# Feed-forward input products: seven block products instead of eight, on one Trainium2 core

## The chip, the cores and the metric

The kernel is one launch on one core of a Trainium2 chip. The metric is the device time of the launch in microseconds, the median of several runs. TensorE (PE) multiplies, VectorE (DVE), ScalarE (ACT) and GpSimd (POOL) work element by element, SyncE (SP) issues the weight transfers.

## What is computed

A two-layer encoder for 512 prompt frames and 64 sample frames, 576 columns in all, of width 1024. Each layer has two feed-forward blocks around a mixer (retention in the first layer, forgetting attention in the second). Only the feed-forward block matters here:

```python
gate, up = jnp.split(rmsnorm(h, g) @ w_in, 2, axis=-1)   # w_in: 1024 x 5632
h = h + 0.5 * (silu(gate) * up) @ w_out                  # w_out: 2816 x 1024
```

There are four such blocks, called ffn1_0, ffn2_0, ffn1_1 and ffn2_1. Before ffn2_0 runs the output product of retention, before ffn1_1 the key and value products (sections k and v), before ffn2_1 the output product of attention (fox_out).

## The kernel before

Activations lie transposed: 128 features on the partitions, the 576 columns (T) along the free axis, eight such tiles for h (KD = 8). A unit is one output tile of 128 features: `unit` (L1543) runs over its kt blocks of 128 inputs, and `product` (L1532) makes three matmuls of 288 columns for each block and column half: low weight by high input, high by low, high by high, because each fp32 value is split into two fp32r parts. A unit of eight blocks is 48 matmuls. A feed-forward block has 44 input units, a gate and an up unit for each of the 22 hidden tiles, and its output units run in two parts (FF_PARTS: 10 and 12 hidden tiles), after the input units of the part.

Per unit SP loads the fp32 tile into `raw` (L459), ACT casts it to `wh` (`split_hi`, L597) when the unit two earlier has left PE, DVE subtracts to get `wl` (`split_lo`, L602), and PE waits for that. `section` (L605) puts these splits two units ahead of each unit's eviction. The evictions of a pair: DVE multiplies the gate by the normaliser `rstd` (L989), ACT applies silu (L650), POOL multiplies by `rstd` (L1437), DVE multiplies with the up unit in PSUM (L993), ACT casts (L652) and DVE subtracts (L996), which gives `acth` and `actl` for the output units. Output units are added into h by `take_h` (L962); in the last part ACT scales h by the next gain (`x_tile`, L639), DVE makes its low part (L917), and POOL sums squares (`sum_squares`, L1411, L1418). PE adds the partitions (L1573), DVE takes the root by Newton steps (`token_rstd`, L920) and PE spreads it (L1582), from within the first units of the next section. Everything is ordered by program order on each engine and by semaphores.

## Time and profile before

| | |
|---|---|
| median of 3 runs | 2560.07 us |
| runs | 2559.99 to 2560.84 us |
| the profiled execution | 2560.84 us, its span 2560.8 us |
| PE busy | 2529.7 us |
| DVE, ACT, POOL busy | 1054.5, 697.4, 338.6 us |

The page gives busy time for each engine and a picture of the span in 40 slices. The durations of single instructions come from the trace; those of matmuls overlap one another, so their cost is read from start to start. Duration and start-to-start differ on DVE and ACT too: an instruction whose waits are met starts before the previous one has ended.

### The profile page before, as it was taken

The numbers are of one execution on the slowest core, as the hardware profiler recorded it, in microseconds if no ns is written. First come the engines' busy times: TensorE is split into PE (matmuls) and PEld (weight loads), VectorE is DVE, ScalarE is ACT, GpSimd is POOL, SyncE is SP. The second block draws the span as 40 slices with busy tenths as digits, with TensorE's granted clock in tenths as the row PEclk, the third lists the DMA queues.
The fourth block names the chain that finished last, engine by engine and source line by source line (L and its number), as shares of the span: only waits on it lengthen the run. The fifth ranks groups of instructions, "written<-read, shape, count | busy, mean of one in ns | idle before, by whom it ended". The sixth has DMA issues, their size and how long they took to land.

```text
span 2560.8 us, 44069 instructions
## 1 busy us (share of the span) xinstructions
PE 2529.7 (99%) x18791; PEld 2459.6 (96%) x18791; DVE 1054.5 (41%) x1556; ACT 697.4 (27%) x994; POOL 338.6 (13%) x266
## 2 busy tenths in 40 slices
PE   8999999999999999999999999999999999999998
PEld 8999999989898989999999999999998789999998
DVE  4333334554545555333333343323335754333332
ACT  4222222121313233222222232212223542212221
POOL 0100113210101103100113211001121021100112
PEclk9999999999999999999999999999999999999998
DMA  5222232222223122322232442322324322322231
GB/s 151 85 81 82 82 103 77 81 79 67 88 66 95 57 69 83 92 80 83 82 103 64 138 115 83 89 77 82 99 78 113 114 76 79 88 78 81 85 104 38
DMA packets 394198, 221.71 MB, mean 87 GB/s; under 512 B 8593, under 2 KB 386545, under 8 KB 394065
## 3 DMA queue, kind: packets, MB, share of 16 engines
q1 hardware_dynamic: 389328, 205.22, 27.8%
q0 software_dynamic: 4544, 14.50, 1.7%
q8 instruction: 106, 1.74, 0.3%
q14 instruction: 28, 0.22, 0.0%
q10 hardware_dynamic: 192, 0.04, 0.0%
HBM read 206.01 MB, written 13.71 MB: 86 GB/s over the span
## 4 chain that ended last, share of the span: by engine, by line
PE 96%; DVE 2%; ACT 1%; DMA 0%; issue 0%; SPq 0%; POOL 0%; ACTq 0%; DVEq 0%; POOLq 0%
PE ps L1536 88%; PE ps L1914 1%; PE ps L1719 1%; PE ps L1705 1%; PE ps L1707 1%; PE ps L1706 1%; PE ps L1942 1%; PE ps L1966 1%; DVE wl L602 0%; PE ps L1819 0%; PE ps L1698 0%; PE ps L1739 0%; DVE xl L917 0%; ACT wh L597 0%; DMA xtok<-in_x_sample 0%; PE ps L1778 0%
## 5 line engine op out<-in xcount | busy, mean ns | idle before, releaser
L602 DVE TENSOR_TENSOR wl<-raw,wh 128x1024 fp32r<-128x1024 f32 (+3 forms) x352 | 446.6, 1269 | 1266.5 <-ACT wh L597 1266.1
L1536 PE MATMUL ps<-xh,wl 128*128 128x288 f32 x4000 | 859.9, 297 | 5.9 <-DVE xl L917 4.1
L1536 PE MATMUL ps<-xh,wh 128*128 128x288 f32 x4000 | 852.1, 294 | 0.0
L1536 PE MATMUL ps<-xl,wh 128*128 128x288 f32 x4000 | 851.9, 294 | 0.0
L597 ACT CAST wh<-raw 128x1024 fp32r<-128x1024 f32 (+3 forms) x352 | 375.8, 1068 | 1146.6 <-PE ps L1536 1145.5
L1536 PEld LDWEIGHTS ps<-xh,wl 128*128 128x128 f32 x4000 | 641.2, 188 | 11.9 <-DVE xl L917 4.8
L1536 PEld LDWEIGHTS ps<-xh,wh 128*128 128x128 f32 x4000 | 642.1, 188 | 0.0
L1536 PEld LDWEIGHTS ps<-xl,wh 128*128 128x128 f32 x4000 | 641.9, 188 | 0.0
L1536 PE MATMUL ps<-actl,wh 128*128 128x288 f32 x1408 | 300.9, 294 | 0.0
L1536 PE MATMUL ps<-acth,wl 128*128 128x288 f32 x1408 | 300.4, 295 | 0.0
L1536 PE MATMUL ps<-acth,wh 128*128 128x288 f32 x1408 | 298.7, 293 | 0.0
L1437 POOL TENSOR_TENSOR rsilu<-silu,rstd 128x576 f32<-128x576 f32 x88 | 125.7, 1429 | 1244.7 <-ACT silu L650 1244.7
L1536 PEld LDWEIGHTS ps<-acth,wh 128*128 128x128 f32 x1408 | 225.2, 188 | 0.0
L1536 PEld LDWEIGHTS ps<-actl,wh 128*128 128x128 f32 x1408 | 224.6, 188 | 0.0
L1536 PEld LDWEIGHTS ps<-acth,wl 128*128 128x128 f32 x1408 | 224.2, 187 | 0.0
L650 ACT ACTIVATE silu<-gate 128x576 f32<-128x576 f32 x88 | 60.4, 686 | 186.3 <-DVE gate L989 186.2
L652 ACT CAST acth<-prod 128x576 f32 (+1 forms) x88 | 59.3, 674 | 183.9 <-DVE prod L993 183.9
L996 DVE TENSOR_TENSOR actl<-prod,acth 128x576 f32 (+1 forms) x88 | 66.7, 758 | 78.2 <-ACT acth L652 78.2
L962 DVE SCALAR_TENSOR_TENSOR h<-ps,h 128x576 f32<-128x576 f32 x104 | 78.0, 750 | 14.3 <-PE ps L1536 14.3
L917 DVE SCALAR_TENSOR_TENSOR xl<-h,gains,xh 128x576 fp32r<-128x576 f32 x56 | 56.5, 1020 | 44.3 <-ACT xh L639 33.0
L1411 POOL TENSOR_TENSOR sq<-h 128x576 f32<-128x576 f32 x37 | 45.4, 1226 | 201.4 <-DVE h L962 201.2
L993 DVE TENSOR_TENSOR prod<-ps,rsilu 128x576 f32<-128x576 f32 x88 | 66.0, 750 | 4.7 <-POOL rsilu L1437 4.7
(247 smaller groups left out, 1667.4 us busy)
## 6 DMA issues: line engine op xcount, KB each, us to landing
raw<-in_ffn_w_in SPq DMA_DIRECT2D x176, 512.0 KB, 3.8
raw<-in_ffn_w_out SPq DMA_DIRECT2D x32, 768.0 KB, 4.8
raw<-in_ret_w_in SPq DMA_DIRECT2D x48, 512.0 KB, 3.9
raw<-in_ffn_w_out SPq DMA_DIRECT2D x32, 640.0 KB, 4.4
raw<-in_ret_w_out SPq DMA_DIRECT2D x32, 256.0 KB, 2.7
raw<-in_fox_w_kvf SPq DMA_DIRECT2D x16, 512.0 KB, 4.0
raw<-in_fox_w_q SPq DMA_DIRECT2D x8, 512.0 KB, 5.4
bias<-cum_scratch SPq DMA_DIRECT2D x16, 256.0 KB, 3.4
```

The source lines that it names most:

```text
L597: nc.scalar.copy(wh[:, s % SPLIT, 0:kt, :], raw[:, s, 0:kt, :]).then_inc(hi_ready, 1)
L602: nc.vector.tensor_tensor(wl[:, s % SPLIT, 0:kt, :], raw[:, s, 0:kt, :], wh[:, s % SPLIT, 0:kt, :].bitcast(F32), ALU.subtract).then_inc(lo ...
L650: nc.scalar.activation(silu[:, s // 2, :], gate[:, s // 2, :], ACT.Silu).then_inc(silu_ready, 1)
L652: nc.scalar.copy(acth[:, 2 * i + s // 2, :], prod[:, s // 2, :]).then_inc(act_hi, 1)
L917: nc.vector.scalar_tensor_tensor(xl[:, j, :], h[:, j, :], gains[:, gain + j:gain + j + 1], xh[:, j, :].bitcast(F32), ALU.mult, ALU.subtrac ...
L962: nc.vector.scalar_tensor_tensor(h[:, j, :], unit_psum(s, ring), scale, h[:, j, :], ALU.mult, ALU.add).then_inc(taken, 1)
L993: nc.vector.tensor_tensor(prod[:, b, :], unit_psum(s, DEEP), rsilu[:, b, :], ALU.mult) \
L996: nc.vector.tensor_tensor(actl[:, 2 * i + b, :], prod[:, b, :], acth[:, 2 * i + b, :].bitcast(F32), ALU.subtract).then_inc(act_ready, 1)
L1411: nc.gpsimd.tensor_tensor(out[:, :], h[:, j, :], h[:, j, :], ALU.mult).then_inc(sq_step, 1)
L1437: nc.gpsimd.tensor_tensor(rsilu[:, b, :], silu[:, b, :], rstd[:, :], ALU.mult) \
L1536: mm = nc.tensor.matmul(out[:, a:z], w, x[:, a:z], start=start and n == 0, stop=stop and n == len(terms) - 1)
L1705: nc.tensor.matmul(out, al, bh, start=start, stop=False)
```

## The change

The gate and up tile of one hidden tile form a 2 x 2 block product: rows gate and up, inner halves the even and the odd input blocks, columns the two halves of 288. It is made by the Winograd form of Strassen's scheme with seven products of 128 x 512 by 512 x 288: 84 matmuls in place of 96, named G11, S2, S1, S3, G12, S4, U22. Four of them need sums of weight quarters (`weight_sums`, DVE), three need sums of input quarters (`x_mix`, DVE). All seven weights of a group are split (`factor_hi` on ACT, `factor_lo` on DVE) into a ring with one place per product, so the part for the next group can be made when PE has left that product of the current one. The products of a group share banks, and PE waits in the group for ACT's copy of G11 and for DVE's sums. The three parts now have 8, 8 and 6 hidden tiles. The gate is multiplied by `rstd` before silu (POOL), the up tile stays without it, and `take_scaled` multiplies by it when an output unit is evicted, in two DVE instructions. During the last four units of the section before, `lead` makes the first group's weights. In the retention section's end, fox_out and the v section the inputs are scaled (`fetch`), mixed and split pair by pair.

```diff
-TA = 288
+TA = T // 2
...
-FF_PARTS = [(0, 10), (10, 12)]
+FF_PARTS = [(0, 8), (8, 8), (16, 6)]
+LAST = len(FF_PARTS) - 1
...
+G11, S2, S1, S3, G12, S4, U22 = range(7)
+ENTRY = [4, 5, 6, 0, 1, 2, 3]
+RING = 7
+BANK = [0, 1, 2, 3, 0, 2, 3]
+SUMS = [S1, S2, S3, S4]
+FACTORS, STEPS = 7, 5
...
+            def load_pair(g, row, src):
+                s = (2 * g + row) % RAW
+                units = next((opening[a] for a in (g, g - 1) if a in opening), None)
+                if units is None:
+                    sp.wait_ge(factor_ready, FACTORS * (g - 2) + U22 + row)
+                elif units:
+                    sp.wait_ge(lo_ready, units - RAW + s + 1)
+                sp.dma_start(raw[:, s, :, :], src).then_inc(pair_in[s], 16)
...
+        def factor_hi(act, g, i):
+            units = opening.get(g)
+            if units is None:
+                act.wait_ge(made, FACTORS * (g - 1) + i + 1)
+            elif units:
+                if i < S3:
+                    act.wait_ge(made, FACTORS * g)
+                    act.wait_ge(unit_done, units - KD + 1)
+                else:
+                    act.wait_ge(unit_done, units - (1 if i < S4 else 0))
+            if i in SUMS:
+                act.wait_ge(sums_ready, 4 * g + SUMS.index(i) + 1)
+            else:
+                act.wait_ge(pair_in[(2 * g + (i == U22)) % RAW], 16 * (g // 2 + 1))
+            nc.scalar.copy(entry(wh, i), source(g, i)).then_inc(fhi_ready, 1)
+        def factor_lo(dve, g, i):
+            dve.wait_ge(fhi_ready, FACTORS * g + i + 1)
+            nc.vector.tensor_tensor(entry(wl, i), source(g, i), entry(wh, i).bitcast(F32), ALU.subtract) \
+                .then_inc(factor_ready, 1)
+        def weight_sums(dve, g, which):
+            a11, a12, a21, a22 = [quarter(g, row, col) for row in range(2) for col in range(2)]
+            s1, s2, s3, s4 = [ws[:, n, :, :] for n in range(4)]
+            for n in which:
+                if n == 0:
+                    dve.wait_ge(pair_in[(2 * g) % RAW], 16 * (g // 2 + 1))
+                    dve.wait_ge(pair_in[(2 * g + 1) % RAW], 16 * (g // 2 + 1))
+                if g:
+                    dve.wait_ge(factor_ready, FACTORS * (g - 1) + SUMS[n] + 1)
+                if n != 2:
+                    dve.wait_ge(sums_ready, 4 * g + n)
+                out, in0, in1, op = ((s1, a21, a22, ALU.add), (s2, s1, a11, ALU.subtract),
+                                     (s3, a11, a21, ALU.subtract), (s4, a12, s2, ALU.subtract))[n]
+                nc.vector.tensor_tensor(out, in0, in1, op).then_inc(sums_ready, 1)
+        def lead_lo(dve, g, which):
+            if which == 0:
+                weight_sums(dve, g, range(4))
+            for f in ((G11, S2, S1), (S3, G12), (S4, U22))[which]:
+                factor_lo(dve, g, f)
+            if which == 2:
+                weight_sums(dve, g + 1, range(4))
...
+            def fetch(n, q, ready, plain=True, rows=range(2)):
+                index = x_index[n, q, plain]
+                for r in rows:
+                    j = 2 * q + r
...
+                    gain = (G_FFN1, G_FFN2)[n % 2] + KD * (n // 2)
+                    nc.scalar.activation(xf[:, index % 2, r, :], h[:, j, :], ACT.Copy, scale=gains[:, gain + j:gain + j + 1]) \
+                        .then_inc(xf_ready, 1)
+            def x_hi(n, q, plain=True, turned=True):
+                index = x_index[n, q, plain]
+                if plain:
+                    act.wait_ge(mixed, mix_before[index] + (2 if turned else 1))
+                    nc.scalar.copy(xh[:, 2 * q:2 * q + 2, :], xf[:, index % 2, :, :]).then_inc(xfhi_ready, 1)
+                if turned:
+                    act.wait_ge(mixed, mix_before[index] + 4)
+                    nc.scalar.copy(xmh[:, q, :, :], mix[:, index % 2, :, :]).then_inc(xfhi_ready, 1)
...
+                    def activated(i):
+                        act.wait_ge(prod_ready, g0 + i + 1)
+                        nc.scalar.copy(acth[:, i, :], up[:, (g0 + i) % 2, :]).then_inc(act_hi, 1)
+                    for i in range(n):
+                        g = g0 + i
+                        more = [g + 1] if i < n - 1 else []
+                        act.wait_ge(made, FACTORS * g + G11 + 1)
+                        if g:
+                            act.wait_ge(stepped, STEPS * (g - 1) + 1)
+                        nc.scalar.copy(p1[:, :], ps[:, 4 * (g % 2) + BANK[G11], 0:TA]).then_inc(p1_ready, 1)
+                        for a in more:
+                            factor_hi(act, a, G11)
+                            factor_hi(act, a, S2)
...
+                        if i:
+                            activated(i - 1)
+                        for a in more:
+                            for f in (S1, S3):
+                                factor_hi(act, a, f)
+                        act.wait_ge(made, FACTORS * g + G12 + 1)
+                        if g >= 2:
+                            act.wait_ge(prod_ready, g - 1)
+                        nc.scalar.copy(gate[:, g % 2, 0:TA], ps[:, 4 * (g % 2) + BANK[G12], 0:TA]).then_inc(gate1_ready, 1)
+                        for a in more:
+                            for f in (G12, S4):
+                                factor_hi(act, a, f)
+                        if not more:
+                            split_hi(act, u1, u1 // 4, 0, n)
+                        act.wait_ge(gate_ready, g + 1)
+                        nc.scalar.activation(gate[:, g % 2, :], gate[:, g % 2, :], ACT.Silu).then_inc(silu_ready, 1)
+                        for a in more:
+                            factor_hi(act, a, U22)
+                    activated(n - 1)
+                    split_hi(act, u1 + 1, u1 // 4, 1, n)
...
+            def x_mix(n, q, plain=True, turned=True):
+                index = x_index[n, q, plain]
+                even, odd, m = xf[:, index % 2, 0, :], xf[:, index % 2, 1, :], mix[:, index % 2, :, :]
+                dve.wait_ge(xf_ready, 2 * index + 2)
+                if turned:
+                    nc.vector.tensor_tensor(m[:, 0, :], even[:, TA:T], even[:, 0:TA], ALU.subtract).then_inc(mixed, 1)
+                nc.vector.tensor_tensor(even[:, TA:T], odd[:, TA:T], even[:, TA:T], ALU.subtract).then_inc(mixed, 1)
+                if turned:
+                    dve.wait_ge(mixed, mix_before[index] + 2)
+                    nc.vector.tensor_tensor(m[:, 1, :], even[:, TA:T], even[:, 0:TA], ALU.add).then_inc(mixed, 1)
+                    dve.wait_ge(mixed, mix_before[index] + 3)
+                    nc.vector.tensor_tensor(m[:, 2, :], odd[:, 0:TA], m[:, 1, :], ALU.subtract).then_inc(mixed, 1)
+            def x_lo(n, q, plain=True, turned=True):
+                index = x_index[n, q, plain]
+                if plain:
+                    dve.wait_ge(xfhi_ready, plain_at[n, q])
+                    nc.vector.tensor_tensor(xl[:, 2 * q:2 * q + 2, :], xf[:, index % 2, :, :],
+                                            xh[:, 2 * q:2 * q + 2, :].bitcast(F32), ALU.subtract).then_inc(xfactor_ready, 1)
+                if turned:
+                    dve.wait_ge(xfhi_ready, mixed_at[n, q])
+                    nc.vector.tensor_tensor(xml[:, q, :, :], mix[:, index % 2, :, :], xmh[:, q, :, :].bitcast(F32),
+                                            ALU.subtract).then_inc(xfactor_ready, 1)
...
+            def take_scaled(u, s, j, gain, ring, held=up):
+                dve.wait_ge(unit_done, u + 1)
...
+                nc.vector.scalar_tensor_tensor(y, unit_psum(s, ring), 0.5, rstd[:, :], ALU.mult, ALU.mult).then_inc(scaled, 1)
+                dve.wait_ge(scaled, n_scaled[0])
+                nc.vector.tensor_tensor(h[:, j, :], h[:, j, :], y, ALU.add).then_inc(taken, 1)
+                if gain is not None:
+                    x_tile(j, gain)
...
+                    def gated(i):
+                        g, b = g0 + i, (g0 + i) % 2
+                        dve.wait_ge(silu_ready, g + 1)
+                        dve.wait_ge(stepped, STEPS * (g + 1))
+                        nc.vector.tensor_tensor(up[:, b, :], up[:, b, :], gate[:, b, :], ALU.mult).then_inc(prod_ready, 1)
+                    def activated(i):
+                        g, b = g0 + i, (g0 + i) % 2
+                        dve.wait_ge(act_hi, g + 1)
+                        nc.vector.tensor_tensor(actl[:, i, :], up[:, b, :], acth[:, i, :].bitcast(F32),
+                                                ALU.subtract).then_inc(act_ready, 1)
+                    for i in range(n):
+                        g, b = g0 + i, (g0 + i) % 2
+                        more = [g + 1] if i < n - 1 else []
+                        norm = part == 0 and i == 0
...
+                        for a in more:
+                            factor_lo(dve, a, G11)
+                        made_to(S2)
+                        dve.wait_ge(p1_ready, g + 1)
+                        if g:
+                            dve.wait_ge(stepped, STEPS * g)
+                        nc.vector.tensor_tensor(u2[:, :], bank(S2), p1[:, :], ALU.add).then_inc(stepped, 1)
+                        for a in more:
+                            factor_lo(dve, a, S2)
+                        made_to(S1)
+                        dve.wait_ge(stepped, STEPS * g + 1)
+                        nc.vector.tensor_tensor(u5[:, :], bank(S1), u2[:, :], ALU.add).then_inc(stepped, 1)
+                        if i:
+                            gated(i - 1)
+                        made_to(S3)
+                        dve.wait_ge(stepped, STEPS * g + 2)
+                        if g >= 2:
+                            dve.wait_ge(act_ready, g - 1)
+                        nc.vector.tensor_tensor(up[:, b, TA:T], bank(S3), u5[:, :], ALU.add).then_inc(stepped, 1)
+                        if norm and roots is not None:
+                            roots()
+                        for a in more:
+                            factor_lo(dve, a, S1)
+                            factor_lo(dve, a, S3)
...
+                        if i:
+                            activated(i - 1)
+                        for a in more:
+                            factor_lo(dve, a, G12)
+                        if i < n - 2:
+                            weight_sums(dve, g + 2, range(3))
+                        if not more:
+                            split_lo(dve, u1, None, 0, n)
+                        if norm and scales is not None:
+                            scales()
+                        made_to(S4)
+                        if g >= 2:
+                            dve.wait_ge(prod_ready, g - 1)
+                        nc.vector.tensor_tensor(gate[:, b, TA:T], bank(S4), u2[:, :], ALU.add).then_inc(stepped, 1)
+                        for a in more:
+                            factor_lo(dve, a, S4)
+                        if i < n - 2:
+                            weight_sums(dve, g + 2, range(3, 4))
+                        made_to(U22)
+                        nc.vector.tensor_tensor(up[:, b, 0:TA], bank(U22), u2[:, :], ALU.add).then_inc(stepped, 1)
+                        for a in more:
+                            factor_lo(dve, a, U22)
+                    gated(n - 1)
+                    activated(n - 1)
+                    split_lo(dve, u1 + 1, None, 1, n)
...
-                    p0 = n_pair[0]
-                    pool.wait_ge(rstd_ready, n_norm[0])
-                    with pool.Fori(0, n // 2) as i:
-                        for b in range(2):
-                            pool.wait_ge(silu_ready, p0 + 2 * i + b + 1)
-                            nc.gpsimd.tensor_tensor(rsilu[:, b, :], silu[:, b, :], rstd[:, :], ALU.mult) \
-                                .then_inc(rsilu_ready, 1)
...
+                    g0 = group0[name, part]
+                    if part == 0:
+                        pool.wait_ge(rstd_ready, n_norm[0])
+                    for g in range(g0, g0 + n):
+                        pool.wait_ge(gate1_ready, g + 1)
+                        pool.wait_ge(stepped, STEPS * g + 4)
+                        nc.gpsimd.tensor_tensor(gate[:, g % 2, :], gate[:, g % 2, :], rstd[:, :], ALU.mult) \
+                            .then_inc(gate_ready, 1)
+                sum_squares(h_taken(first[f"{name}_out{LAST}"]), KD - 1 if name == "ffn2_1" else KD)
...
+            def factor_block(n, g, b, i, q):
+                out = ps[:, 4 * b + BANK[i], 0:TA]
+                e = 4 * ENTRY[i] + q
+                terms = ((wl[:, e, :], x_factor(n, True, i, q)), (wh[:, e, :], x_factor(n, False, i, q)),
+                         (wh[:, e, :], x_factor(n, True, i, q)))
+                for m, (w, x) in enumerate(terms):
+                    mm = nc.tensor.matmul(out, w, x, start=i < G12 and q == 0 and m == 0, stop=q == QUADS - 1 and m == 2,
+                                          skip_group_check=i in (G12, S4, U22))
+                if q == QUADS - 1:
+                    mm.then_inc(made, 1)
+            def factor_arrives(g, i):
+                pe.wait_ge(factor_ready, FACTORS * g + i + 1)
+                if not (isinstance(g, int) and g < 2) and i in (G11, S1, S3):
+                    pe.wait_ge(*((gate1_ready, g - 1) if i == G11 else (stepped, STEPS * (g - 2) + (4 if i == S1 else 5))))
+                if i == G12:
+                    pe.wait_ge(p1_ready, g + 1)
+                if i in (S4, U22):
+                    pe.wait_ge(stepped, STEPS * g + (2 if i == S4 else 3))
...
+            def factors(name, part, norm=False, arrives=None, midway=None):
+                n, g0, groups = FFNS.index(name), group0[name, part], FF_PARTS[part][1]
+                units = opening[g0]
+                if units:
+                    pe.wait_ge(taken, units if name == "ffn1_1" and part == 0 else units - 2)
+                if part == 0:
+                    for q in range(QUADS):
+                        if arrives is not None:
+                            arrives(q)
+                        if q == QUADS - 1 and midway is not None:
+                            midway()
+                        for i in (G11, S2, S1, S3):
+                            if q == 0:
+                                factor_arrives(g0, i)
+                            pe.wait_ge(xfactor_ready, x_factor_at(n, i, q))
+                            factor_block(n, g0, 0, i, q)
+                    group(n, g0, 0, begin=G12)
+                    if norm:
+                        spread_rstd(SPREAD_AT, 6)
+                else:
+                    group(n, g0, 0)
...
+                with pe.Fori(1, groups // 2) as a:
+                    for b in range(2):
+                        group(n, g0 + 2 * a + b, b)
...
```

## Rows read from the trace of the kernel before

**Rows 1.** The page: busy times, and the granted clock in tenths, 40 slices.
```profile
PE 2529.7 (99%) x18791; PEld 2459.6 (96%) x18791; DVE 1054.5 (41%) x1556; ACT 697.4 (27%) x994; POOL 338.6 (13%) x266
PEclk9999999999999999999999999999999999999998
```
**Rows 2.** DVE in order of time: start, duration, instruction (gates of ffn1_0, splits of ffn2_1).
```profile
105.17 0.75 DVE L989 TENSOR_TENSOR gate<-ps,rstd 128x576 f32<-128x576 f32 x1
117.97 0.75 DVE L989 TENSOR_TENSOR gate<-ps,rstd 128x576 f32<-128x576 f32 x1
...
2323.17 1.23 DVE L602 TENSOR_TENSOR wl<-raw,wh 128x1024 fp32r<-128x1024 f32 x1 [4.34 <-ACT wh L597]
2329.41 1.23 DVE L602 TENSOR_TENSOR wl<-raw,wh 128x1024 fp32r<-128x1024 f32 x1 [4.34 <-ACT wh L597]
```
**Rows 3.** Groups by line and shape: count, busy us, mean ns, idle before.
```profile
L996 DVE TENSOR_TENSOR actl<-prod,acth 128x576 f32 x56 | 42.5, 758 | 54.5 <-ACT acth L652 54.5
L1090 DVE TENSOR_TENSOR sTl<-sT,sTh 128x512 fp32r<-128x512 f32 x4 | 2.7, 678 | 0.1
L1096 DVE TENSOR_TENSOR sT<-ps,dm 128x256 f32<-128x256 f32 x4 | 1.6, 408 | 0.0
L597 ACT CAST wh<-raw 128x512 fp32r<-128x512 f32 x32 | 19.8, 619 | 88.6 <-PE ps L1536 88.6
L652 ACT CAST acth<-prod 128x576 f32 x56 | 37.7, 674 | 115.6 <-DVE prod L993 115.6
L853 ACT COPY pt<-ps 128x256 f32<-128x256 f32 x16 | 6.0, 374 | 0.9
L1437 POOL TENSOR_TENSOR rsilu<-silu,rstd 128x576 f32<-128x576 f32 x88 | 125.7, 1429 | 1244.7 <-ACT silu L650 1244.7
```
**Rows 4.** In order of time, one hand-over in retention's output: DVE, then ACT.
```profile
946.14 0.69 DVE L602 TENSOR_TENSOR wl<-raw,wh 128x512 fp32r<-128x512 f32 x1 [1.86 <-ACT wh L597]
946.75 0.75 DVE L962 SCALAR_TENSOR_TENSOR h<-ps,h 128x576 f32<-128x576 f32 x1
948.35 0.82 DVE L917 SCALAR_TENSOR_TENSOR xl<-h,gains,xh 128x576 fp32r<-128x576 f32 x1 [0.85 <-ACT xh L639]
...
947.54 0.78 ACT L639 ACTIVATE xh<-h,gains 128x576 fp32r<-128x576 f32 x1 [1.43 <-DVE h L962]
```
**Rows 5.** In order of time, DVE and POOL at work together.
```profile
455.22 0.76 DVE L1048 TENSOR_TENSOR rt<-rt,const 128x576 f32<-128x576 f32 x1
455.89 1.98 DVE L1050 TENSOR_TENSOR rt<-rt,const 128x576 f32<-128x576 f32 x1
963.52 0.74 DVE L962 SCALAR_TENSOR_TENSOR h<-ps,h 128x576 f32<-128x576 f32 x1
...
455.27 1.98 POOL L1454 TENSOR_TENSOR rt<-rt,const 128x576 f32<-128x576 f32 x1 [10.50 <-DVE rt L1036]
963.13 1.76 POOL L1418 TENSOR_TENSOR ssq<-ssq,sq 128x576 f32<-128x576 f32 x1
```
**Rows 6.** The chain that ended last: start, us, what.
```profile
36.34 0.97 PE ps L1582 x4
443.47 1.20 PE ps L1573 x10
978.02 8.86 PE ps L1536 x54
2127.51 1.06 PE ps L1536 x6
```
**Rows 7.** Stretches: us, then busy us (count) of each engine, granted clock, DMA share, GB/s.
```profile
975.00:978.00 3.00, 0.00 (x0) 0.00 (x0) 2.13 (x2) 1.35 (x2) 2.84 (x3) 0.97 0.59 174
978.00:980.00 2.00, 1.98 (x8) 1.98 (x9) 0.00 (x0) 0.05 (x1) 1.24 (x1) 0.50 0.01 2
1955.00:1960.00 5.00, 2.97 (x25) 2.60 (x25) 4.20 (x21) 4.79 (x17) 0.00 (x0) 1.00 0.00 2
```
**Rows 8.** The page, DMA issues: KB each, median us from issue to landing.
```profile
raw<-in_ffn_w_in SPq DMA_DIRECT2D x176, 512.0 KB, 3.8
```

More of the change, by code:

```diff
@@ L594, in split_hi @@
             act.wait_ge(raw_ready[s], 16 * q + 16)
[L595 removed]
+            g = closing.get(u - u % 4, None) if isinstance(u, int) and u % 4 < SPLIT else None
+            if g is not None:
+                act.wait_ge(made, FACTORS * (g - 1) + (G12 if u % 4 == 0 else U22) + 1)
+            else:
                 act.wait_ge(unit_done, u - SPLIT + 1)
[L597 removed]
+            nc.scalar.copy(slot(wh, s, kt), raw[:, s, 0:kt, :]).then_inc(hi_ready, 1)
@@ new lines, in lead_lo, with lead_hi, section @@
+        def lead_lo(dve, g, which):
[5 more added lines that the diff above has]
+                weight_sums(dve, g + 1, range(4))
+        def lead_hi(act, g, which):
+            for f in ((G11, S2, S1), (S3, G12), (S4, U22))[which]:
+                factor_hi(act, g, f)
+        def section(eng, name, split, take, after_first=None, ahead=None, lead=None):
@@ L617, in four @@
                         split_at(s + 2)
+                    if last and s and lead is not None and then is not None:
+                        lead(eng, then, s - 1)
                     if start and s == 0:
@@ new lines, in settled, with units @@
+            def settled(name, part, u):
+                g = group0[name, part] + FF_PARTS[part][1]
+                if u < 4:
+                    pe.wait_ge(stepped, STEPS * (g - 1 + u // 2))
+                    pe.wait_ge(gate1_ready, g - 1 + u // 2)
+            def units(name, mh, ml, arrives, before_unit):
+                u0, kt = first[name], blocks[name]
+                for j in range(KD):
+                    before_unit(j)
+                    unit(u0 + j, j % 4, kt, mh, ml, arrives if j == 0 else None, DEEP)
```

480 lines of the change are left out of this document (277 added, 203 removed).

## The prediction

> **What bounds the kernel now.** I read the page first: PE is busy for 2529.7 of 2560.8 us and its granted clock is full almost everywhere, while DVE works 41% of the time, ACT 27%, POOL 13% [rows 1]. So a matmul less is 0.13 us less, as long as the other engines keep up. Then the order of time inside a feed-forward block: from gate to gate, that is two units or 96 matmuls, 12.80 us pass in the first part, 0.1333 us for a matmul; in the second part a unit takes 6.24 us, 12.48 us for a pair [rows 2]. DVE needs 2 x 1.2 for splits, 2 x 0.75 for gate and product and 0.76 for the low part, some 4.7 us of each pair [rows 2, 3], so it has 8 us to spare. Last, the chain that ended last and the stretches tell how the blocks begin: DVE, not PE, is late there [rows 6, 7].
>
> **What is removed.** 12 of 96 matmuls for each of 88 hidden tiles. A group of 84 takes PE 84 x 0.1333 = 11.2 us. The 22 pairs of a block take 10 x 12.80 + 12 x 12.48 = 277.8 us now; 22 groups at 11.2 are 246.4. That is 31.4 us for a block, 126 us in all, if nothing else ends later. The output units keep their 1056 matmuls.
>
> **What is added to each group on DVE.** Its in-order round for group g (the loop in the diff) holds: seven low parts and four weight sums, each 128x512 from two SBUF tiles; five half-tile sums of 288 columns from PSUM; the product `gated` and the low part `activated`, 576 columns each. Prices: a 512 pass takes 0.68 to 0.69 us, and the next instruction starts 0.61 after it [rows 3, 4]; a 256 column pass from PSUM 0.41, so 288 columns some 0.44 and 0.36 to the next start; a 576 pass 0.76, 0.67 to the next [rows 3]. Sum: 11 x 0.605 + 5 x 0.36 + 2 x 0.67 = 9.8 us. Against 11.2 that still fits. Three things come on top:
>
> (a) POOL. When POOL multiplies from SBUF, a DVE pass with two SBUF inputs stands still: the second `rt` product took 1.98 us where the first took 0.76, and it ended 0.6 us after POOL's instruction, which itself had first waited for DVE's previous one (it ran 1.27 us from 455.98) [rows 5]. They take turns. A pass with an input in PSUM took 0.74 beside a busy POOL, so it isn't held [rows 5]. Now POOL's product is covered: it runs when DVE is idle, 1.43 us each [rows 3]. After the change it starts when DVE has made the gate's second half, and next on DVE stand S4's low part and the fourth weight sum: the sum waits until POOL is done, 1.2 us.
>
> (b) ACT and DVE wait for each other. A hand-over costs 0.03 to 0.04 us [rows 4], but the work between is serial. I walk one round from the end of the gate's second half (0). S4's low part ends at 0.6, POOL's product at 1.9, silu (priced as ACT's other 576 pass, 0.67, rows 3) at 2.6, U22's high part (0.62, 0.52 to the next) at 3.1; DVE has finished the sum and the half of up by 2.8 and starts U22's low part at 3.2: 0.45 lost. ACT copies G11 (0.4) and casts G11's weights by 3.96; DVE starts their low part at 4.0, 0.2 lost. Then U2, S2's low part, U5, `gated`, ending at 6.7; only now may ACT cast acth (0.67) and after it S1's weights, done at 7.9; DVE has only one half-tile sum meanwhile and starts S1's low part at 7.95, 1.0 lost. S3, `activated`, G12, three sums (the second needs the first: 0.1) and the gate's half end at 12.8.
>
> So a round is 9.8 + 1.2 + 0.45 + 0.2 + 1.0 + 0.1 = 12.8 us. In the round PE has 11.2 us of work: DVE and its two partners set the pace. PE's waits are for ACT's copy of G11 and for U5. The weights' arrival isn't in it: SP may load after U22's low part, the next sums come some 6.6 us later, a load lands in 3.8 us, two in a row in more [rows 8].
>
> Not every group pays. The first group of a part finds its weights made, n groups have n - 1 rounds, and a round may begin 3.1 us late before PE feels it (U5 is ready 5.4 us into a group at best and needed at 8.0, and in a late round comes 2.0 us after the round's start, so the start can slip from 2.9 to 6.0). A part of eight loses 7 x 1.6 - 3.1 = 8.1 us, one of six 4.9: 21.1 for a block. Of the 31.4 us, 10.3 remain, **41 us in the four blocks**.
>
> **What the trace doesn't show** is a DVE pass over weight quarters with a stride, and a loop of such hand-overs. Below, I bound the round by busy time alone with POOL's turn, 11.1 us (all of ACT hidden); above, by 0.1 us more at each of six hand-overs, 13.4 us. I take 12.8, since the hand-overs of rows 4 are of the same unrolled kind. One tenth of a us in the round is worth 76 rounds x 0.1 = 7.6 us.
>
> A rule of the skill bears on (a). The Trainium skill, GPSIMD Engine Reference, 1. Specifications, says that GpSimd's interfaces to SBUF are shared with VectorE, and that VectorE instructions with two SBUF inputs, or in a two-port mode, contend. The trace agrees [rows 5].
>
> Without the taking of turns POOL would end at 1.55 in the walk and the round would be 12.5 us, 26 us less in all.
>
> **Starts of the blocks.** Now: PE's first block runs as if it had begun at 17.9 us (at 36.34 it had done 138 matmuls) [rows 6]. After: DVE must, in order, copy four tiles (2.7), mix four pairs (four half passes each, two of them waiting for the one before: 1.9), make low parts of 1152 and 864 columns for each pair (2.25), seven low parts and eight sums of weights (9.2): 28.5 us, with about 3 us of waits for ACT, from about 9 us on. It comes to its first round at 40, to the root at 46, since ACT squares the last tiles in that round, and PE may spread it at 49 and starts group 1 at 50; now the same point is 17.9 + 11.2 + 1.0 = 30. **+20 us.**
>
> ffn2_0: retention's output units take PE only 3.2 us each. In that time DVE gets, beside split and eviction, half a mixing and low parts (2.1 us), then in the last three units seven low parts and eight sums (9.2 us), while POOL adds squares from the fifth tile on and every SBUF pass of DVE waits for its turn (1.2 us for some twelve of them). I walk it to the last tile's mixing at 19 us behind now: PE has the last quarter of the inputs some 60 us after the first of the eight units instead of the 36 or so of now. Now PE waits there too, 3.0 us, then 54 matmuls run in 8.86 instead of 7.2 us, because the clock was granted at half [rows 6, 7]; that comes again. **+22 us.**
>
> ffn2_1: the units of fox_out take 6.4 us. After the last one DVE still has, in order: S3 and G12, the eviction of tile 6, S4 and U22, whose place is free only now, four sums, the eviction of tile 7, then scaling, mixing, low parts: 17 us, and group 0's rest 6. PE has 12.2 us of work for it. **+10 us** (now 1.3, the wait before 2127.51 [rows 6]). ffn1_1: most mixing lies ahead in the v section, the same S4, U22 and sums stand before the last eviction: **+5 us.**
>
> The new root chain (2 us of DVE in the first round of three blocks): +6.
>
> **Ends of the blocks.** `take_scaled` adds a 576 pass from SBUF to each output unit, 0.7 us. In parts 0 and 1 (6.4 us units) it is covered. In the last part a unit now takes PE 4.8 us, not 9.6, and DVE needs split 0.9, two passes 1.5, the wait for ACT 0.85 and x's low part 0.8, with POOL's two products taking turns 1.2 each: 5.5 us. The lag grows over the units and reaches the first unit of the next section, which needs the last tile at 5.6 us: I get 4.3 us late, three times, **+13 us**. The last block's tail: the extra pass, +1.
>
> **Sum.** 2560 - 41 + 20 + 22 + 10 + 5 + 6 + 13 + 1 = **2596 us**; the profiled execution's own time, 2560.84, is 0.8 above the median, which I leave out.
>
> **Rivals.**
> 1. PE stays the bound, faster. ACT's casts come early enough and a round is 11.1 us: 126 us saved, and 36 off the sum's other terms, since starts are then caught up partly: 2560 - 126 + 60 = about 2495. It decides below a round of 12.3 us (36 / 7.6 tenths under 12.8): from there the kernel is faster, whatever the starts cost. For it: DVE's busy sum, 9.8, fits. Against: the order of ACT's loop, in which acth's cast stands before S1's. Chance 0.18. A milder form, a round of 12.5 and starts at two thirds of my price, gives 2560 - 64 + 51 = 2547; chance 0.13.
> 2. Dearer hand-overs, 13.4 us: +46, 2640. Chance 0.12.
> 3. The weights come late: a sum waits for its transfer, since SP's load stands behind U22's low part. A us per round is +76, 2670. Rows 8 give 3.8 us against 6.6; chance 0.04.
> 4. The clock. PE has gaps of 0.7 and 1.0 us in each round. After 3.0 us without a matmul it was granted at half; in a stretch with 2.97 of 5 us busy it stayed full [rows 7]. If each gap brought back 3 us at half, a round would grow by up to 1.5 us: 2700. Chance 0.03. The Trainium skill, TensorE: Matmul & The Clock Gate, Part 1, says that the clock is gated to half when the array has been idle; the trace agrees for the long gap, and not for the short ones.
> That the products aren't what they say is no rival: the matmuls are in the code one by one.
>
> **How the numbers follow.** My forecast, 2560 to 2635, has 0.5. Range: from 2525, which takes in the milder form of rival 1, to 2645 with the dearer hand-overs. Below 0.2% (5 us) nothing can be told from no change. Faster: 0.18 + 0.13, slightly less for its part near zero, 0.30. Same 0.05. Slower 0.65.
>
> **What would show it.** In a middle group of a part: the period from one S1 low part to the next (12.8, or 11.2); the DVE's idle time before S1's and U22's low parts, ended by ACT; one weight sum per group at 1.8 us; PE waiting before G12 and S4. At the starts: the first matmul after the first spread at 50 us, and over 8 us of idle PE before ffn2_0. I am wrong if the periods are 11.2, or if the order lets ACT run ahead.

## The result and the profile after

The changed kernel takes 2632.64 us (median; 2629.73 to 2633.23), the kernel before, run beside it, 2560.45. The ratio is 1.0278, 95% interval [1.0263, 1.0292]: slower, by 72 us where the forecast said 36. The profiled execution has a span of 2630.5 us; its page shows less work on PE (2469.0 us for 2529.7 in [rows 1]) and 743 us more on DVE.

```profile
PE 2469.0 (94%) x17735; PEld 2364.6 (90%) x17735; DVE 1797.3 (68%) x2930; ACT 934.3 (36%) x1680; POOL 358.6 (14%) x266
PEclk9999999999999998999999989999999998999998
L1763 POOL TENSOR_TENSOR gate<-gate,rstd 128x576 f32<-128x576 f32 x88 | 149.0, 1693 | 1374.7 <-DVE gate L1286 1374.7
```

The same executions in order of time. First POOL's product of the gate (start, duration, instruction, idle time before it and who ended it). It is there once per group, so its starts mark the rounds: they are 12.83 and 12.85 us apart.

```profile
81.70 1.74 POOL L1763 TENSOR_TENSOR gate<-gate,rstd 128x576 f32<-128x576 f32 x1 [11.10 <-DVE gate L1286]
94.53 1.74 POOL L1763 TENSOR_TENSOR gate<-gate,rstd 128x576 f32<-128x576 f32 x1 [11.10 <-DVE gate L1286]
107.38 1.74 POOL L1763 TENSOR_TENSOR gate<-gate,rstd 128x576 f32<-128x576 f32 x1 [11.10 <-DVE gate L1286]
```

Then part of a round on DVE, from the gate's second half of one group on, and below it PE's two waits in it:

```profile
119.62 0.45 DVE L1286 TENSOR_TENSOR gate<-ps,u 128x288 f32<-128x288 f32 x1
119.99 0.68 DVE L704 TENSOR_TENSOR wl<-ws,wh 128x512 fp32r<-128x512 f32 x1
120.70 1.80 DVE L721 TENSOR_TENSOR ws<-raw,ws 128x512 f32<-128x512 f32 x1
122.43 0.45 DVE L1292 TENSOR_TENSOR up<-ps,u 128x288 f32<-128x288 f32 x1
123.21 1.51 DVE L704 TENSOR_TENSOR wl<-raw,wh 128x512 fp32r<-128x512 f32 x2 [0.34 <-ACT wh L699]
...
127.98 1.29 DVE L704 TENSOR_TENSOR wl<-ws,wh 128x512 fp32r<-128x512 f32 x2 [0.89 <-ACT wh L699]
```
```profile
123.53 0.40 PE L1917 MATMUL ps<-xh,wl 128*128 128x288 f32 x1 [0.43 <-ACT p L811]
126.11 0.40 PE L1917 MATMUL ps<-xh,wl 128*128 128x288 f32 x1 [0.73 <-DVE u L1258]
```

It is the walk of the prediction nearly to the tenth: the fourth weight sum at 1.80 us while POOL multiplies, U22's low part waiting 0.34 for ACT, S1's 0.89, PE waiting before G12 and S4. From the first gate product of part 0 of ffn1_0 to that of part 1 148.9 us pass; TensorE's own work in it is 8 x 11.2 + 51.2 = 140.8, so the part loses 8.1.

Where the 72 us stand is read from four marks that both kernels have: the matmuls that add the sums of squares over the partitions, once behind each of the first three blocks, and the end.

| up to | before | after | later | share of this section | forecast |
|---|---|---|---|---|---|
| end of ffn1_0 | 443.41 | 463.00 | 19.6 | 19.6 | 20 + 2 - 10.3 + 4.3 = 16.0 |
| end of ffn2_0 | 1401.18 | 1442.24 | 41.1 | 21.5 | 22 + 2 - 10.3 + 4.3 = 18.0 |
| end of ffn1_1 | 1940.26 | 2000.63 | 60.4 | 19.3 | 5 - 10.3 + 4.3 = -1.0 |
| end | 2560.8 | 2630.5 | 69.7 | 9.3 | 10 + 2 - 10.3 + 1 = 2.7 |

The third row holds more than half of the miss. This is PE at the end of the v section and the start of ffn1_1, and what DVE did meanwhile:

```profile
1563.14 0.71 PE L2198 MATMUL ps<-const,kvt 128*128 128x128 f32 x5
1577.29 0.61 PE L1917 MATMUL ps<-xh,wl 128*128 128x288 f32 x1 [13.45 <-DVE kvt L1591]
```
```profile
1571.22 1.36 DVE L1140 TENSOR_TENSOR xl<-xf,xh 128x1152 fp32r<-128x1152 f32 x1 [1.27 <-ACT xh L792]
1572.49 0.68 DVE L704 TENSOR_TENSOR wl<-ws,wh 128x512 fp32r<-128x512 f32 x1
1573.10 0.68 DVE L704 TENSOR_TENSOR wl<-raw,wh 128x512 fp32r<-128x512 f32 x1
1573.70 0.68 DVE L721 TENSOR_TENSOR ws<-raw 128x512 f32<-128x512 f32 x1
...
1576.49 0.75 DVE L1591 TENSOR_TENSOR kvt<-ps,rstd 128x576 f32<-128x576 f32 x1
```

v's last unit has left PE by 1563; its eviction starts at 1576.49, behind four pairs of mixes and low parts (3.07 us each, DVE and ACT in turn), two low parts and four weight sums. Then the clock: stretches after the wait (length, then busy us and count of PE, PEld, DVE, ACT and POOL, then granted clock as a share of the full one, DMA share, GB/s).

```profile
1577.00:1582.00 5.00, 4.71 (x20) 4.71 (x21) 0.24 (x1) 0.00 (x0) 0.00 (x0) 0.51 0.41 111
1582.00:1587.00 5.00, 5.00 (x40) 5.00 (x40) 0.37 (x1) 1.96 (x5) 0.56 (x1) 1.00 0.00 0
```

Twenty matmuls start in the first stretch and forty in the second. The clock is at half from the first matmul at 1577.3 to 1581.9 us, 4.6 us in which half the work is done: 2.3 us more.

### The profile page after: what moved, and what is told of

Same layout as the page of the kernel before. It is cut to its first block and busy times, and to the rows that moved or that the text cites. A ratio compares the mean times of both kernels' runs of the same rounds, so it can differ in the third digit from the quotient of the medians.

```text
span 2630.5 us, 44796 instructions
## 1 busy us (share of the span) xinstructions
PE 2469.0 (94%) x17735; PEld 2364.6 (90%) x17735; DVE 1797.3 (68%) x2930; ACT 934.3 (36%) x1680; POOL 358.6 (14%) x266
## 5 line engine op out<-in xcount | busy, mean ns | idle before, releaser
L681 DVE TENSOR_TENSOR wl<-raw,wh 128x1024 fp32r<-128x1024 f32 (+2 forms) x208 | 253.5, 1219 | 483.3 <-ACT wh L676 483.3
L676 ACT CAST wh<-raw 128x1024 fp32r<-128x1024 f32 (+2 forms) x208 | 197.7, 950 | 581.4 <-PE ps L1861 581.4
L1917 PEld LDWEIGHTS ps<-xh,wl 128*128 128x128 f32 x1408 | 267.6, 190 | 125.0 <-DVE u L1258 50.1
L1917 PE MATMUL ps<-xmh,wl 128*128 128x288 f32 x1056 | 315.3, 299 | 0.9 <-DVE xml L1144 0.6
L1917 PE MATMUL ps<-xmh,wh 128*128 128x288 f32 x1056 | 315.5, 299 | 0.0
L1917 PE MATMUL ps<-xml,wh 128*128 128x288 f32 x1056 | 315.1, 298 | 0.0
L704 DVE TENSOR_TENSOR wl<-ws,wh 128x512 fp32r<-128x512 f32 x352 | 235.7, 690 | 79.5 <-ACT wh L699 79.4
L1917 PEld LDWEIGHTS ps<-xl,wh 128*128 128x128 f32 x1408 | 268.0, 190 | 0.2
L1917 PEld LDWEIGHTS ps<-xh,wh 128*128 128x128 f32 x1408 | 267.5, 190 | 0.0
L699 ACT CAST wh<-ws 128x512 fp32r<-128x512 f32 x352 | 210.1, 618 | 121.0 <-PE ps L1861 53.1
```

The lines of the kernel that those rows point to most:

```text
L676: nc.scalar.copy(slot(wh, s, kt), raw[:, s, 0:kt, :]).then_inc(hi_ready, 1)
L681: nc.vector.tensor_tensor(slot(wl, s, kt), raw[:, s, 0:kt, :], slot(wh, s, kt).bitcast(F32), ALU.subtract).then_inc(lo_ready, 1)
L699: nc.scalar.copy(entry(wh, i), source(g, i)).then_inc(fhi_ready, 1)
L704: nc.vector.tensor_tensor(entry(wl, i), source(g, i), entry(wh, i).bitcast(F32), ALU.subtract) \
L1917: mm = nc.tensor.matmul(out, w, x, start=i < G12 and q == 0 and m == 0, stop=q == QUADS - 1 and m == 2, skip_group_check=i in (G12, S4, U22))
```

## The experiments

The theory has three parts: (1) a round is a walk through hand-overs between DVE, ACT and POOL; (2) an opening is late by what DVE has queued before the last tile; (3) the last part's output units are lifted over PE's 4.8 us. The rival to (1) is that DVE's throughput alone sets the round, so that no order matters; to (2) and (3), that a lag at a start or an end is hidden. All were timed beside the kernel before.

**cast_late.** ACT's loop:

```diff
-                        if i:
-                            activated(i - 1)
                         for a in more:
                             for f in (S1, S3):
                                 factor_hi(act, a, f)
+                        if i:
+                            activated(i - 1)
```

> The changed kernel, but ScalarE casts the activated tile (acth) after the weight casts of S1 and S3 instead of before them; VectorE's order is untouched. Theory (the round of 12.84 us is a walk through hand-overs between VectorE and ScalarE, and ScalarE's order costs 1.0 us of it): the idle time of VectorE before S1's low part (0.89 us) goes, the period of the rounds in the middle of a part falls to 12.0 (11.85 to 12.2), and the kernel comes to 2572 us (2557 to 2580), 52 to 76 under 2633. Rival A (the round is VectorE's throughput: busy time and its turns with GpSimd, so order is worth nothing): period 12.8, 2633 us. Rival B (the wait moves to the low part of the activated tile, which now waits for the same cast): period 12.5 or more, over 2605 us.

Measured: 2579.96 us, ratio 1.0078 [1.0061, 1.0095]; the period is 11.86:

```profile
66.06 1.74 POOL L1763 TENSOR_TENSOR gate<-gate,rstd 128x576 f32<-128x576 f32 x1 [10.12 <-DVE gate L1286]
77.91 1.75 POOL L1763 TENSOR_TENSOR gate<-gate,rstd 128x576 f32<-128x576 f32 x1 [10.12 <-DVE gate L1286]
```

One exchanged pair of casts gives 53 us: the order is in the round, and the wait didn't move elsewhere. The time lies at the upper edge of the expected range, because the size depends on how many rounds are long. 0.99 us in 76 rounds would be 75 us. But the last two rounds of each part, whose groups have fewer weights to make, were never long (10.84 and 9.63 us in the changed kernel, 9.86 and 10.61 here, the same sum). 5 rounds in a part of eight and 3 in one of six are 52; 52 x 0.99 = 51.5.

**cast_late_u22_early.** As above, and `factor_hi(act, a, U22)` stands ahead of the wait for `gate_ready` and silu.

> As cast_late, and ScalarE also casts U22's weights before silu instead of after it. Theory of the hand-overs: 0.3 to 0.45 us more of each round goes (the wait before U22's low part), period 11.6 to 11.8, 2565 us (2548 to 2572). Rival A (VectorE's throughput): 12.8 and 2633. Rival C (silu, now 0.6 later, becomes what the product waits for): no gain over cast_late.

Measured: 2549.37 us, ratio 0.9954 [0.9937, 0.9971], period 11.34, under the 11.6 to 11.8 expected, and 31 us less again. It is now 0.5% faster than the kernel before. DVE waits for no other engine in a round any more; its longest idle time is 0.10 us, between two weight sums of which one needs the other. In these stretches (columns as above), the first of the changed kernel, the second of this one, DVE goes from 46.0 to 51.1 of 52 us busy, and PE has no wait left:

```profile
64.00:116.00 52.00, 47.45 (x343) 45.60 (x342) 46.00 (x74) 22.96 (x47) 6.96 (x4) 1.00 0.28 81
```
```profile
64.00:116.00 52.00, 52.00 (x389) 51.47 (x388) 51.13 (x83) 24.96 (x50) 8.69 (x5) 1.00 0.30 87
```

**pool_tiny.** `gate[:, g % 2, 0:8]` by `rstd[:, 0:8]` on POOL.

> The changed kernel with GpSimd's product of the gate by the normaliser cut to 8 of the 576 columns; the gate is otherwise not normalised, so a part of the computation is left out. The orders of the other engines are untouched. Theory (VectorE stands still for 1.2 us while GpSimd multiplies, and silu comes 1.3 us later for it): one weight sum per round falls from 1.80 to 0.69 us, period 11.5 to 11.8, 2556 us (2545 to 2575). Rival (the stand-still only fills time in which VectorE would wait for ScalarE anyway): period over 12.5, over 2607 us. If only the taking of turns mattered and not the wait for silu, the forecast's own figure, 12.5, would come: 2607 us.

Measured: 2552.74 us, ratio 0.997 [0.9959, 0.998], period 11.62. The fourth sum takes 0.69 us, and the wait for ACT before U22's low part is still there:

```profile
112.40 0.69 DVE L721 TENSOR_TENSOR ws<-raw,ws 128x512 f32<-128x512 f32 x1
113.01 0.45 DVE L1292 TENSOR_TENSOR up<-ps,u 128x288 f32<-128x288 f32 x1
113.69 0.69 DVE L704 TENSOR_TENSOR wl<-raw,wh 128x512 fp32r<-128x512 f32 x1 [0.23 <-ACT wh L699]
```

So POOL's product costs 1.2 us of a round with ACT's old order: 1.11 are the fourth sum's, and the wait is 0.11 shorter. The edit takes away the turn and silu's delay at once, so it doesn't tell them apart. It gives 80 us, not 52 x 1.22 = 63, because the last round but one of each part shrinks too (from 10.84 to 9.62 us): 64 rounds x 1.22 = 78.

**orders_pool_tiny.** Both edits together.

> cast_late_u22_early with GpSimd's product of the gate by the normaliser cut to 8 columns, so the gate is otherwise not normalised. It asks what bounds the round of 11.34 us. Theory (VectorE without any idle time, 10.15 us of passes and 1.2 of standing still for GpSimd): VectorE drops to 10.2 us and TensorE's 84 matmuls take over at 84 x 0.1333 = 11.2 us; 0.14 us less in some 68 rounds and the block ends of parts earlier, 2540 us (2534 to 2545). Rival (a round of matmuls costs more than 11.2 us, since TensorE switches products): period 11.3, 2547 to 2551.

Measured: 2541.01 us, ratio 0.9922 [0.9905, 0.9939], periods around 11.15. DVE is busy 48.9 of 52 us, PE all 52: TensorE is the bound at 84 x 0.1333 = 11.2. The first two rounds of ffn1_0, in which DVE is still catching up with PE, show DVE's own pace without POOL's product: 10.08 and 10.13 us. In cast_late_u22_early DVE waits for nobody, so the 1.2 us between 10.1 and 11.34 are POOL's turn alone. From 11.34 down to 11.15 DVE was the bound, with that turn in it.

**v_take_first.** DVE takes v's last tile before it mixes the last two pairs and before the last lead.

```diff
-                    if last and s and lead is not None and then is not None:
+                    late = name == "v" and lead is lead_lo
+                    if last and s and lead is not None and then is not None and not (s == 3 and late):
                         lead(eng, then, s - 1)
...
                     take(i, s)
+                    if last and s == 3 and lead is not None and then is not None and late:
+                        lead(eng, then, 2)
...
-                    if n == 2 * KD - 2:
-                        for q in range(QUADS):
+                    if n >= 2 * KD - 2:
+                        for q in range(2 * (n % 2), 2 * (n % 2) + 2):
```

> The changed kernel, but at the end of the v section VectorE takes the last tile of v (kvt) before it mixes the last two pairs of the inputs and before S4, U22 and the four sums, instead of after them. Theory (TensorE waits 13.45 us at the start of ffn1_1 for that eviction alone, and then runs on at half clock for some us): the wait falls to about 4 us and the kernel comes to 2624 us (2620 to 2627), 6 to 13 under 2633. Rival (the low parts of the inputs, which come at the same times as before, hold group 0 just as long): 2633, within 2 us.

Measured: 2623.44 us, ratio 1.0247 [1.023, 1.0264], 9.2 us less. DVE's S4 and U22 come within 0.5 us of their old times (1572.98 for 1572.49), the sums within 1; the eviction has moved by 10.2 us:

```profile
1566.25 0.75 DVE L1594 TENSOR_TENSOR kvt<-ps,rstd 128x576 f32<-128x576 f32 x1
```
```profile
1567.05 0.40 PE L1920 MATMUL ps<-xh,wl 128*128 128x288 f32 x1 [3.39 <-DVE kvt L1594]
```

**lead_late.** With that, `lead_lo(dve, g, 2)` and `lead_hi(act, g, 2)` (S4, U22, four sums) come after the last tile's addition, mix and split at ffn2_0 and ffn2_1 too.

> v_take_first, and the same order at the two other openings: in the last output unit of retention (before ffn2_0) and of fox_out (before ffn2_1) VectorE and ScalarE take the last tile of h, scale, mix and split it before they make S4, U22 and the four sums, which group 0 and group 1 need later. In the changed kernel these six passes (4.9 us from 2189.19 to 2194.43) stand between tile 6 and tile 7. Theory (each opening is late by what VectorE has queued before the last tile): 4 to 5 us less at each of the two, 2614 us (2611 to 2617) where v_take_first gave 2623.4. Rival (group 0 now waits for S4 and U22 instead): no gain over v_take_first, 2621 to 2625.

Measured: 2616.53 us, ratio 1.0216 [1.0199, 1.0233]: 6.9 us less than v_take_first where 9 was expected. In the profiles ffn2_0's end gains 6.7 (1436.86 for 1443.51), of which 1.3 were there at the end of ffn1_0, where the two kernels are still alike; so some 5 us are ffn2_0's opening and 2 ffn2_1's. At ffn2_1 the mixes of the last tile now fall together with POOL's sum of squares and take turns with it (below: 1.58, 1.40, 1.54 us for passes of 0.46):

```profile
2173.94 1.41 DVE L1208 SCALAR_TENSOR_TENSOR h<-ps,h 128x576 f32<-128x576 f32 x2
2176.20 1.58 DVE L1132 TENSOR_TENSOR mix<-xf 128x288 f32<-128x288 f32 x1 [0.84 <-ACT xf L788]
2177.71 1.40 DVE L1133 TENSOR_TENSOR xf<-xf 128x288 f32<-128x288 f32 x1
2179.14 1.54 DVE L1136 TENSOR_TENSOR mix<-xf 128x288 f32<-128x288 f32 x1
```

**one_pass_last.** `take_scaled` gives way to `take_h(..., 0.5, gain, DEEP)` in three last parts.

> The changed kernel, but the output units of each of the three last parts are added into h in one VectorE instruction without the normaliser of up, as in the kernel before; multiplying by it there is left out. Theory (the second pass of 0.76 us is what lifts the unit over TensorE's 4.8 us): unit period 4.8 us, 4.3 us less at three ends, 2620 us (2617 to 2623). Rival (GpSimd's squares, not the second pass, hold the unit up): period 5.2 or more, less than 6 us gained, over 2627.

Measured: 2613.40 us, ratio 1.02 [1.0183, 1.0217], 19 us less where 13 was expected. The first three marks come 5.0, 9.6 and 16.4 us earlier. But 2.9 of the last difference are there before v has ended (PE's wait in v ends at 1542.08 for 1554.58): PE ran at half clock behind the second mark (clock 0.57 from 1441 to 1449 us), and here it doesn't (1.00 from 1432 to 1440). So the three ends are worth 5.0, 7.5 and 3.9. In the changed kernel DVE's unit is 5.5 us (439.21 to 444.68):

```profile
439.21 2.17 DVE L681 TENSOR_TENSOR wl<-raw,wh 128x768 fp32r<-128x768 f32 x1
441.31 0.74 DVE L1195 SCALAR_TENSOR_TENSOR up<-ps,rstd 128x576 f32<-128x576 f32 x1
442.09 0.76 DVE L1197 TENSOR_TENSOR h<-h,up 128x576 f32<-128x576 f32 x1
443.69 1.06 DVE L1119 SCALAR_TENSOR_TENSOR xl<-h,gains,xh 128x576 fp32r<-128x576 f32 x1 [0.85 <-ACT xh L773]
444.68 2.18 DVE L681 TENSOR_TENSOR wl<-raw,wh 128x768 fp32r<-128x768 f32 x1
```

With one pass it is 4.80 (433.28 to 438.08, each split at 0.96): POOL's work is then over when the split starts (438.10).

**x_low_deferred.** DVE makes x's low part one unit later (`x_tile(n - 1, gain)` ahead of `take_scaled`).

> The changed kernel, but in the last part's output units of ffn1_0, ffn2_0 and ffn1_1 VectorE makes the low part of x one unit later, after the next unit's weight split, so that it doesn't idle 0.85 us for ScalarE's cast. Theory (a unit takes VectorE 5.47 us and TensorE 4.8, the lag reaches the next section): the unit falls to 4.8 us, the wait of 2.17 us in the next section's first unit goes, 4.3 us less at each of three ends, 2620 us (2617 to 2623). Rival (the lag is hidden, since the next section's units give it back): 2633, within 2 us.

Measured: 2639.28 us, ratio 1.0301 [1.0283, 1.0318]: 6.6 us slower, against both expectations. The wait of 0.85 is gone and one of 1.57 is there, for ACT's split of the weights, which on ACT stands behind the cast of x, which waits for the addition:

```profile
438.80 2.05 DVE L681 TENSOR_TENSOR wl<-raw,wh 128x768 fp32r<-128x768 f32 x1 [1.57 <-ACT wh L676]
440.77 0.81 DVE L1119 SCALAR_TENSOR_TENSOR xl<-h,gains,xh 128x576 fp32r<-128x576 f32 x1
...
444.60 2.05 DVE L681 TENSOR_TENSOR wl<-raw,wh 128x768 fp32r<-128x768 f32 x1 [1.57 <-ACT wh L676]
```

**x_both_deferred.** ACT's cast is deferred in the same way.

> x_low_deferred with ScalarE's cast of x deferred as well: in the last part's output units of three blocks both engines first split the next unit's weights and then make the high and low part of the tile of x before. Theory (x_low_deferred put the split behind the cast of x on ScalarE and so made one chain of addition, cast, split and low part, 5.80 us per unit; the lag of the changed kernel itself is worth 5.5 us at each end, as one_pass_last showed): VectorE has 4.4 us of work per unit, the unit falls to 4.8 us, 5 us less at each of three ends, 2617 us (2614 to 2621). Rival (the chain through GpSimd's squares holds the unit up whatever the order): 2628 to 2640.

Measured: 2621.71 us, ratio 1.0233 [1.0216, 1.025], 11 us less than the changed kernel, not 16. The waits for ACT are shorter, but two passes of a unit take turns with POOL now:

```profile
433.94 1.48 DVE L681 TENSOR_TENSOR wl<-raw,wh 128x768 fp32r<-128x768 f32 x1 [0.63 <-ACT wh L676]
435.33 1.99 DVE L1120 SCALAR_TENSOR_TENSOR xl<-h,gains,xh 128x576 fp32r<-128x576 f32 x1
```

This unit lasts 4.80 us all the same (433.94 to 438.74), as the theory said. What is still late is the last tile: its low part starts at 458.94, 1.7 us before that of the changed kernel (460.61) and 3.4 behind that of one_pass_last (455.58), and in each unit before it two DVE passes are still stretched (at 454.48 one of 0.81 to 1.70, at 456.89 one of 0.76 to 1.21). That POOL's turns are what is missing is read from these rows; no run isolates it.

**all_orders** (both cast orders, lead_late, x_low_deferred) and **orders_mended** (the same with x_both_deferred).

> cast_late_u22_early, lead_late and x_low_deferred together; everything is computed as in the changed kernel. Theory (the terms are separate places and add up): 2549.4 less 9 (v), 9 to 10 (two openings) and 13 (block ends), 2518 us (2512 to 2526), 42 us under the kernel before. Rival (what is won at a start or an end is given back because VectorE, busy without a gap in a round of 11.34 us, sets the pace there too): 2530 to 2545.

> all_orders with ScalarE's cast of x deferred as in x_both_deferred; everything is computed. Theory (the places add up: cast_late_u22_early 2549.4, lead_late 16.1 less, block ends 16 less): 2517 us (2512 to 2524), 43 us under the kernel before. Rival: as all_orders, 2535 to 2542.

Measured: all_orders 2539.39 us, ratio 0.9915 [0.9899, 0.9932]; orders_mended 2524.82, ratio 0.9864 [0.9847, 0.988]. The single results add up: 2549.4 - 16.1 + 6.6 = 2539.9, and 2549.4 - 16.1 - 10.9 = 2522.4. At most 2.4 us are given back, less than the single runs of x_both_deferred lie apart (2618.74 to 2624.73). orders_mended ended just above its range, all_orders missed its expectation by what x_low_deferred had missed. orders_mended computes all that the changed kernel does, with the same instructions in another order, and is 35 us under the kernel before and 108 under the changed one.

## Why the prediction was right and wrong

The time, 2633 us, lies inside the range, 2525 to 2645, and the direction is right. But the range went up for dearer hand-overs, which did not come; what filled it were dearer openings and ends, so that it holds is luck. The account, term by term:

- **The round: right.** 12.8 forecast, 12.84 measured, with each of its waits in place, and the two edits that the walk names took out 0.99 (of 1.0) and 0.52 (of 0.45). The loss of a part of eight was forecast as 8.1 and is 8.1, though for a reason half wrong: "7 x 1.6 - 3.1" counts seven long rounds and a slack, the trace shows five long ones (5 x 1.6 = 8). At 12.8 both give the same; at 11.86 the first gives 7 x 0.66 - 3.1 = 1.5, the second 3.3. cast_late follows the second (198.24 - 54.23 - 140.8 = 3.2). It is no general rule either: in pool_tiny, period 11.62, a part loses 0.8 (195.43 - 53.86 - 140.8) and not 5 x 0.42 = 2.1, since a sixth round got shorter. So "one tenth of a us in the round is worth 76 rounds" should have been 52 for a wait like that of S1, 5.2 us, and 64 for POOL's turn.
- **POOL's turn: right** in size (1.80 for 0.69 us). The Trainium skill, SBUF — State Buffer, section "SBUF: two separate sides", calls the pair of ports that DVE and GpSimd share an exclusive lock, held for the whole instruction; the traces agree, in lead_late even with three short mixes in a row.
- **"ffn1_1: +5 us": the step that failed.** Its sign and its queue were named ("the same S4, U22 and sums stand before the last eviction"), its size was not worked out, and no group 0 can cover it, since PE asks for that eviction before the first matmul of the block (in `factors`). Measured: PE starts ffn1_1 13.45 us after v's last work, then 2.3 us at half clock; v itself ends 1563.85 - 1516.03 = 47.8 us late where the mark before it had 41.1. Of these 6.7, 2.8 arise right behind the mark, at k's start, and belong to the end of ffn2_0 (below); the other 3.9 are a wait of 2.12 us for an eviction that stands behind mixing (at 1554.58) and the half clock after it. In all 3.9 + 13.45 + 2.3 = 19.7 for 5. v_take_first took 9.2 of it away.
- **ffn2_1: +10** was short as well: 9.3 + 10.3 - 2 - 1 = 16.6, with 1.2 of the output units' pace (below) in it. The six passes before tile 7 were in the list; what was left out is that POOL's last sum of squares, for which PE waits 6.36 us at 2198.09, comes only then, and the half clock of both waits (the other is 2.80 us, at 2186.62).
- **ffn1_0: +20 and ffn2_0: +22**: with 7.1 for the end of a block, the first two rows leave 20.8 and 22.7: right. PE spreads the root at 51.0, the forecast said 49.
- **Ends: +4.3 each** was short, and the half clock behind them was put at nothing. From the first of the last part's 288 output matmuls to the first matmul of the next section PE takes 41.4 us (412.7 to 454.15) for 288 x 0.1333 = 38.4: 3.0 late, 2.17 of it one wait. From there to the mark it is 8.8 us for 6.4 before, with the clock at 0.50 from 455.5 to 458.9. That is 5.4 for an end, and behind the second mark the half clock takes 2.8 more. The unit's own 5.5 us was met (5.47) by luck: the terms listed add up to 0.9 + 1.5 + 0.85 + 0.8 + 2 x 1.2 = 6.45, but the rows show one turn of 1.2 (a split of 2.17 for 0.96) and only 0.25 of the second (1.06 for 0.81).
- **"The output units keep their 1056 matmuls"** holds for their number, not for their pace: in the kernel before 480 of them take 63.5 us (from 147.6 us on, 0.1322 each), in the changed one 384 take 51.2 (from 140.6 us on, 0.1333 each), 1.2 us for a block. Why the pace differs is open. The third row needs 7.1 for the end of a block (19.3 - 19.7 - 2.8 + 10.3): 5.4 + 1.2, and half a us is left.
- The misses add up to 14.7 (ffn1_1) + 6.6 (ffn2_1) + 0.8 + 0.7 (the first two openings) + 3 x 2.8 (ends with the pace) + 2.8 (behind the second mark) = 34.0 of the 36.6; the rest is the difference between the profiled spans and the medians. 23 of it are openings.
- **The rivals.** PE as the bound (2495) needed ACT's casts early: the order of ACT's loop, named as the reason against it, was the reason. Its 2495 doesn't follow from its own words: the other terms are 77, and 36 off them leaves 41, not 60. That two moved lines would bring the round from 12.84 to 11.34, DVE being busy without a gap, was not seen. The clock stayed full through the waits of 0.43 and 0.73 us: 1.00 in the stretch from 64 to 116 us.

What stays open: the output units' pace, whether PE must ask for v's last eviction before the first matmul of ffn1_1 at all, and how much of ffn2_0's opening (waits of 7.1, 4.1 and 6.3 us in the changed kernel) another order could win; lead_late took some 5 us of it.

## What to carry to other kernels

When a change moves work from the bounding engine to three others that hand it to one another, the sum of their busy times (9.8 us here) says little: walk one period with every wait, and then ask of each wait whether the instruction ahead of it could stand behind it. Count how many periods really are of full length. At a seam between two stages, write down the queue of the engine that evicts the last tile, item by item, with what PE asks for before its first matmul; here the seam whose queue was named but not worked out held the largest error.

## What the runs showed of the hardware that was not expected

- After a wait of 3.39 us PE began at full clock (matmuls of 0.40, then 0.29 us) and fell to half (0.44) one us later, for 3.4 us; the stretch in v_take_first:

```profile
1567.00:1571.00 4.00, 3.95 (x19) 3.95 (x20) 2.16 (x3) 2.97 (x4) 0.00 (x0) 0.62 0.00 0
```

  After 13.45 us it was at half from the first matmul. The Trainium skill, TensorE: Matmul & The Clock Gate, "Part 1: The HAM clock gate", names an idle TensorE as what halves the clock. The trace agrees for both waits, and for shorter ones: half clock followed waits of 2.17 us (454.15) and 2.12 us (1554.58) too. What sets how late the drop comes isn't shown by any run here.
- POOL instructions in a row hold up one DVE pass after another: in x_both_deferred, with two POOL products per unit, two DVE passes of 0.96 and 0.81 us took 1.48 and 1.99. Moving a pass out of a wait for ACT put it into a wait for POOL.
